# Weight split in 256-column pieces, sign folded into a selecting block, fewer input transfers, mean scaled on ScalarE, later value blocks first

## What is computed

```python
# stick-breaking: weights of a block of queries times the values
a = jnp.where(causal, jnp.exp(jax.nn.log_sigmoid(z) + rest), 0.0)
o = jnp.einsum('bhqk,bhkd->bhqd', a, v)
...
# matrix memory, gates: running sum b, and the running maximum of ig - b
b = jnp.cumsum(lfc, axis=-1)
log_d = b[..., :, None] - b[..., None, :] + igc[..., None, :]
m_t = jnp.maximum(jnp.max(log_d, axis=-1), log_inter)
d = jnp.exp(log_d - m_t[..., None])
...
def layer_norm(x, g, b):
    mu = jnp.mean(xf, axis=-1, keepdims=True)
    var = jnp.mean(jnp.square(xf - mu), axis=-1, keepdims=True)
    return (xf - mu) * lax.rsqrt(var + LN_EPS) * g + b
...
for i in range(2):
    x = layer_norm(ALPHA * x + mix, ...)
    x = layer_norm(ALPHA * x + jnp.square(jax.nn.relu(x @ w_up)) @ w_down, ...)
    x = x + jax.nn.sigmoid(x @ ple_w_gate + ple_b_gate) * (p @ ple_w_proj)
```

## Time and profile before

| | |
|---|---|
| median of 3 runs | 1488.28 us (1486.82 to 1488.86) |
| profiled execution | 1491.34 us, its span 1489.2 us |
| TensorE (PE) busy | 1475.4 us, 99% |
| VectorE (DVE) | 707.4 us, 48% |
| ScalarE (ACT) | 434.9 us, 29% |
| GpSimd (POOL) | 901.6 us, 61% |
| mean granted clock of TensorE | 0.999 |

### The profile page before, as it was taken

The page is one execution under the profiler, slowest core; times in us unless marked ns, Lnnn a source line. Parts: engine busy times, 40 slices in busy tenths (PEclk is TensorE's granted clock), DMA queues, the critical chain, the costliest instruction groups (busy, mean ns, idle before and its releaser), DMA issues.

```text
span 1489.2 us, 19731 instructions
## 1 busy us (share of the span) xinstructions
PE 1475.4 (99%) x7141; PEld 1198.9 (81%) x7150; DVE 707.4 (48%) x868; ACT 434.9 (29%) x880; POOL 901.6 (61%) x719
## 2 busy tenths in 40 slices
PE   9999999999999999999999999999999999999999
PEld 6888677878878888888888888877888888888887
DVE  6674658260036676103541183677777300552253
ACT  3242665141123422001210053766152100221032
POOL 7766035486633597667776656810659666777653
PEclk9999999999999999999999999999999999999999
DMA  6323011232221333333233322310323333333322
GB/s 207 113 86 107 16 43 62 80 113 84 89 69 43 99 99 110 93 94 98 99 99 99 95 65 96 123 35 15 99 68 116 99 99 94 93 97 99 99 85 85
DMA packets 37891, 132.72 MB, mean 89 GB/s; under 512 B 4368, under 2 KB 4800, under 8 KB 37824
## 3 DMA queue, kind: packets, MB, share of 16 engines
q1 hardware_dynamic: 37296, 130.39, 27.6%
q10 hardware_dynamic: 528, 1.36, 0.3%
HBM read 129.59 MB, written 2.10 MB: 88 GB/s over the span
## 4 chain that ended last, share of the span: by engine, by line
PE 94%; DVE 2%; ACT 2%; DMA 1%; POOL 0%; issue 0%; DVEq 0%; SPq 0%; ACTq 0%; POOLq 0%
PE PS L644 22%; PE PS L645 22%; PE PS L646 22%; PE PS L595 3%; PE PS L596 3%; PE PS L577 3%; PE PS L822 2%; PE PS L669 1%; PE PS L670 1%; PE PS L671 1%; PE PS L1099 1%; PE PS L914 1%; PE PS L929 1%; DMA W_raw<-in_weights 1%; PE PS L784 1%; PE PS L786 1%
## 5 line engine op out<-in xcount | busy, mean ns | idle before, releaser
L536 POOL TENSOR_TENSOR W_lo<-W_raw,W_hi 128x1024 fp32r<-128x1024 f32 x238 | 601.0, 2525 | 19.9
L533 POOL TENSOR_TENSOR HOLD<-HOLD 1x1 f32<-1x1 f32 x238 | 61.9, 260 | 550.9 <-PE PS L646 307.2
L644 PE MATMUL PS<-A_hi,W_hi 128*128 128x512 f32 x904 | 352.6, 390 | 0.0
L645 PE MATMUL PS<-A_hi,W_lo 128*128 128x512 f32 x904 | 351.9, 389 | 0.0
L646 PE MATMUL PS<-A_lo,W_hi 128*128 128x512 f32 x904 | 351.9, 389 | 0.0
L534 POOL TENSOR_SCALAR W_hi<-W_raw 128x1024 fp32r<-128x1024 f32 x238 | 247.3, 1039 | 0.0
L644 PE MATMUL PS<-H_hi,W_hi 128*128 128x512 f32 x512 | 199.2, 389 | 0.0
L645 PE MATMUL PS<-H_hi,W_lo 128*128 128x512 f32 x512 | 199.2, 389 | 0.0
L646 PE MATMUL PS<-H_lo,W_hi 128*128 128x512 f32 x512 | 199.2, 389 | 0.0
L644 PEld LDWEIGHTS PS<-A_hi,W_hi 128*128 128x128 f32 x904 | 170.0, 188 | 35.8 <-DVE A_lo L1733 0.5
L646 PEld LDWEIGHTS PS<-A_lo,W_hi 128*128 128x128 f32 x904 | 169.8, 188 | 35.4
(11 more groups left out here) (347 smaller groups left out, 2037.2 us busy)
## 6 DMA issues: line engine op xcount, KB each, us to landing
W_raw<-in_weights SPq DMA_DIRECT2D x238, 512.0 KB, 3.5
X<-in_x SPq DMA_DIRECT2D x8, 256.0 KB, 5.9
out<-X SPq DMA_DIRECT2D x7, 256.0 KB, 4.1
RELU<-in_ple_in ACTq DMA_DIRECT2D x2, 512.0 KB, 3.7
CONST<-in_constants SPq DMA_DIRECT2D x1, 849.5 KB, 8.8
PARAM<-in_params SPq DMA_DIRECT2D x1, 320.5 KB, 7.3
SIN<-in_positions ACTq DMA_DIRECT2D x1, 256.0 KB, 4.0
out<-X SPq DMA_DIRECT2D x2, 128.0 KB, 1.7
```

The lines of the kernel that those rows point to most:

```text
L533: pool.tensor_tensor(HOLD[:, 1 + s:2 + s], HOLD[:, 0:1], HOLD[:, 0:1], ALU.add)
L536: pool.tensor_tensor(W_lo[:, s, :], W_raw[:, r, :], W_hi[:, s, :].bitcast(F32), ALU.subtract).then_inc(w_lo, 1)
L644: pe.matmul(PS[:, bank, :], W_hi[:, slot, w], hi[:, kk, :], start=first, stop=False)
L645: pe.matmul(PS[:, bank, :], W_lo[:, slot, w], hi[:, kk, :], start=False, stop=False)
```

## The change

- `split`: the copy to `W_hi` and the subtraction to `W_lo` are each issued as four instructions of 256 columns (`W_PIECES`); the semaphores are set by the last piece.
- `X_PARTS` is 4 instead of 8: `X` comes in four transfers of two tiles each.
- Stick-breaking: a new semaphore `sb_att_later` is set after the exponential of blocks 1 to 3. TensorE waits for it first, multiplies blocks 1, 2, 3, then waits for `sb_att` and multiplies block 0.
- Layer norm: VectorE leaves the sum over features unscaled in `SMALL[:, 44:48]` and signals `tokens_summed`, for which it waits itself too; ScalarE scales it to the mean between `projected(0)` and `projected(1)` and signals `mean_held`; L2148 is gone. TensorE spreads the mean before `project(l, half, 2, 1)` instead of after it.
- Gates: `SELECT_B` is the block times -1, and `ROWS[:, 2, :]` is not negated any more.

```diff
--- before.py
+++ after.py
@@ -45,7 +45,8 @@
 QK_SCALE = HD ** -0.5
 NEG = -1e30
 RAW_SLOTS, W_SLOTS = 2, 4
-X_PARTS = 8
+W_PIECES = [slice(c * D // 4, (c + 1) * D // 4) for c in range(4)]
+X_PARTS = 4
 WOVEN = 3
 ACC = 4
 
@@ -305,7 +306,7 @@
         stats_done, mean_ready = sem("stats_done"), sem("mean_ready")
         var_ready, sd_ready = sem("var_ready"), sem("sd_ready")
         rstd_cols, rstd_ready = sem("rstd_cols"), sem("rstd_ready")
-        mean_cols, mean_held = sem("mean_cols"), sem("mean_held")
+        mean_cols, mean_held, tokens_summed = sem("mean_cols"), sem("mean_held"), sem("tokens_summed")
 
         centred, normed, x_ready, x_home = sem("centred"), sem("normed"), sem("x_ready"), sem("x_home")
         act_own, dve_own = sem("act_own"), sem("dve_own")
@@ -325,6 +326,7 @@
         angle_ready, angle_done = sem("angle_ready"), sem("angle_done")
 
         qk_sq, qk_lo, qk_ms, qk_sd, qk_normed = (sem("qk_" + n) for n in ("sq", "lo", "ms", "sd", "normed"))
+        sb_att_later = sem("sb_att_later")
         head_mean_in, minus_in = sem("head_mean_in"), sem("minus_in")
 
         fox_soft, fox_rows, fox_gates_in = sem("fox_soft"), sem("fox_rows"), sem("fox_gates_in")
@@ -531,10 +533,13 @@
                     pool.wait_ge(block_done, n - W_SLOTS + 1)
 
                 pool.tensor_tensor(HOLD[:, 1 + s:2 + s], HOLD[:, 0:1], HOLD[:, 0:1], ALU.add)
-                pool.tensor_scalar(W_hi[:, s, :], W_raw[:, r, :], 1.0, 1.0, ALU.mult, ALU.mult).then_inc(w_hi, 1)
+                for c in W_PIECES:
+                    done = pool.tensor_scalar(W_hi[:, s, c], W_raw[:, r, c], 1.0, 1.0, ALU.mult, ALU.mult)
+                done.then_inc(w_hi, 1)
                 pool.wait_ge(w_hi, n + 1)
-                pool.tensor_tensor(W_lo[:, s, :], W_raw[:, r, :], W_hi[:, s, :].bitcast(F32),
-                                   ALU.subtract).then_inc(w_lo, 1)
+                for c in W_PIECES:
+                    done = pool.tensor_tensor(W_lo[:, s, c], W_raw[:, r, c], W_hi[:, s, c].bitcast(F32), ALU.subtract)
+                done.then_inc(w_lo, 1)
 
             pool.memset(HOLD[:], 0.0).then_inc(hold_set, 1)
             pool.wait_ge(hold_set, 1)
@@ -1019,12 +1024,14 @@
                     add(SP_lo, 0).then_inc(sb_summed, 1)
 
                 def weigh(c):
-                    pe.wait_ge(sb_att, 2 * c + 2)
-                    for j in range(NT):
+                    pe.wait_ge(sb_att_later, 2 * c + 2)
+                    for j in (1, 2, 3, 0):
+                        if j == 0:
+                            pe.wait_ge(sb_att, 2 * c + 2)
                         for h in (2 * c, 2 * c + 1):
                             half = slice(h % 2 * HD, h % 2 * HD + HD)
                             mm = pe.matmul(PS[half, 6 + c, j * P:T], V1[:, j, 4 + c, half], packed(ATT, h % 2, j),
-                                           start=j == 0, stop=j == NT - 1, skip_group_check=True)
+                                           start=j == 1, stop=j == 0, skip_group_check=True)
                     mm.then_inc(sb_weighed, 1)
 
                 late = PLAN["late1"].before
@@ -1136,9 +1143,9 @@
                 turn_sums(SQSUM, 5).then_inc(stats_done, 1)
                 project(l, half, 1, 1)
                 project(l, half, 2, 0)
-                project(l, half, 2, 1)
                 pe.wait_ge(mean_held, n + 1)
                 spread_columns(MEAN_AT, 4).then_inc(mean_ready, 1)
+                project(l, half, 2, 1)
                 spread_rstd(n + 1)
                 project(l, half, 3, 0)
                 project(l, half, 3, 1)
@@ -1432,7 +1439,7 @@
                 def weights(h):
                     later = slice(PACKED_AT[1], PACKED)
                     act.wait_ge(sb_summed, 2 * h + 1)
-                    act.activation(ATT[:, h % 2, later], packed_scores(h)[:, later], ACT.Exp)
+                    act.activation(ATT[:, h % 2, later], packed_scores(h)[:, later], ACT.Exp).then_inc(sb_att_later, 1)
                     act.wait_ge(sb_summed, 2 * h + 2)
                     act.activation(packed(ATT, h % 2, 0), packed_scores(h, 0), ACT.Exp).then_inc(sb_att, 1)
 
@@ -1582,6 +1589,8 @@
                     act.activation(projection(4 * (n % 2) + i), PS[:, PROJECTION_BANKS[i], :], ACT.Copy).then_inc(by_act, 1)
 
                 projected(0)
+                act.wait_ge(tokens_summed, n + 1)
+                act.activation(SMALL[:, MEAN_AT:MEAN_AT + NT], SMALL[:, 44:48], ACT.Copy, scale=1.0 / D).then_inc(mean_held, 1)
                 projected(1)
                 act.wait_ge(var_ready, n + 1)
                 act.activation(SMALL[:, RSTD_AT:RSTD_AT + NT], SMALL[:, 56:60], ACT.Sqrt, bias=EPS_COL[:, 1:2]).then_inc(sd_ready, 1)
@@ -2126,7 +2135,7 @@
                     add_square_to(KD - 1)
 
             def layer_norm(n, stage_at):
-                mean, square, var = SMALL[:, MEAN_AT:MEAN_AT + NT], SMALL[:, 52:56], SMALL[:, 56:60]
+                total, square, var = SMALL[:, 44:48], SMALL[:, 52:56], SMALL[:, 56:60]
 
                 def scaled_low(k):
                     dve.wait_ge(x_ready, KD * n + k + 1)
@@ -2136,16 +2145,18 @@
                     dve.tensor_tensor(X[:, k, :], X[:, k, :], PS[:, 4, :], ALU.subtract).then_inc(centred, 1)
 
                 dve.wait_ge(mean_cols, n + 1)
-                own(dve.tensor_reduce(mean, PS[:, 7, :].rearrange("p (t c) -> p t c", t=NT), mybir.AxisListType.X, ALU.add))
+                dve.tensor_reduce(total, PS[:, 7, :].rearrange("p (t c) -> p t c", t=NT), mybir.AxisListType.X,
+                                  ALU.add).then_inc(tokens_summed, 1)
+                dve.wait_ge(tokens_summed, n + 1)
                 dve.wait_ge(stats_done, n + 2)
                 own(dve.tensor_reduce(var, PS[:, 5, :].rearrange("p (t c) -> p t c", t=NT), mybir.AxisListType.X, ALU.add))
                 own.wait()
-                own(dve.scalar_tensor_tensor(out=square, in0=mean, scalar=1.0 / (D * D), in1=mean, op0=ALU.mult, op1=ALU.mult))
+                own(dve.scalar_tensor_tensor(out=square, in0=total, scalar=1.0 / (D * D), in1=total, op0=ALU.mult,
+                                             op1=ALU.mult))
                 own.wait()
                 own(dve.scalar_tensor_tensor(out=var, in0=var, scalar=1.0 / D, in1=square, op0=ALU.mult, op1=ALU.subtract))
                 own.wait()
                 dve.tensor_scalar(var, var, 0.0, None, ALU.max).then_inc(var_ready, 1)
-                dve.tensor_scalar(mean, mean, 1.0 / D, None, ALU.mult).then_inc(mean_held, 1)
                 reciprocal_columns(n + 1)
                 dve.wait_ge(mean_ready, n + 1)
                 centre(0)
@@ -2206,7 +2217,7 @@
             def memory_gates():
                 fg = slice(32, 32 + M_HEADS)
                 own(dve.memset(PARTS_B[:], 0.0))
-                own(dve.tensor_copy(SELECT_B[:], const("select", row=slice(0, 68))))
+                own(dve.tensor_scalar(SELECT_B[:], const("select", row=slice(0, 68)), -1.0, None, ALU.mult))
                 dve.wait_ge(m_tanh, 1)
                 dve.tensor_scalar(MG[:, 2, :], MG[:, 1, :], CAP, None, ALU.mult).then_inc(m_capped, 1)
                 dve.wait_ge(m_soft, 1)
@@ -2220,9 +2231,6 @@
                 own(dve.tensor_tensor_scan(ROWS[:, 2, :], ROWS[:, 0, :], ROWS[:, 0, :], 0.0, ALU.max, ALU.max))
                 own.wait()
                 dve.tensor_tensor(ROWS[:, 3, :], ROWS[:, 1, :], ROWS[:, 2, :], ALU.add).then_inc(m_rows, 1)
-                dve.wait_ge(m_rows, 1)
-                own(dve.tensor_scalar(ROWS[:, 2, :], ROWS[:, 2, :], -1.0, None, ALU.mult))
-                own.wait()
                 own(dve.tensor_copy(PARTS_B[0:M_HEADS, :], ROWS[:, 2, :]))
                 own.wait()
                 own(dve.tensor_tensor(REST[fg, :], ROWS[:, 2, :], PARTS_B[0:M_HEADS, :], ALU.subtract))
```

## The result

The changed kernel takes 1502.93 us (median of 4 runs, 1502.68 to 1503.03) against 1488.57 (1486.82 to 1489.03) for the kernel before: ratio 1.0091, 95% interval 1.0078 to 1.0105. It is 14 us slower, where 5 us faster was forecast. The profiled execution has a span of 1501.2 us, 12.0 more than before.

A forecast was written before the change was run, and what follows sets the result against it. TensorE, busy 99% of the span, was taken as the bound, so only its standstills count: -4.1 - 1.1 - 0.4 + 0 + 0.3 = -5.3 us, giving 1483.0 us, range 1481.0 to 1487.3.

The forecast's parts named there:

- The split in pieces of 256 columns: GpSimd's weight split: six more instructions add 0.9 us a block, about 4.55 against TensorE's 5.44, hidden behind the matmuls.
- first MLP halves: Where VectorE and GpSimd exclude each other: a block takes 5.3 to 5.4 of 5.44 us, just covered, costed at nothing.
- rival A: First MLP halves: GpSimd becomes the bound at 0.26 us a piece, 15 us lost over 24 blocks, 1493 us; chance 9%.
- Gate stage: TensorE's wait for PARTS_B and the half clock behind it go once the negation is out: -4.1 us, bounds 1.2 to 4.1.
- Rival D: Gate stage: the stall stays, the chain only waits for the same POOL instructions; 1.2 instead of 4.1, 1485.9 us; chance 6%.
- +0.3 for the third weight block: Gate stage, woven start of qk2: the third block, needed three tiles later, costs 0.3 us, bounds 0 and 1.8.
- rival B: Gate stage: the stall moves to a weight block, 1.8 us instead of 0.3, 1484.5 us, 1486.2 if the clock falls; 16%.
- Norms: Four normalisations: spreading the mean one product earlier saves 0.27 us each, 1.1 us in all, bounds nothing to 1.6.
- Stick-breaking: TensorE's wait for the weights ATT: multiplying the later blocks first saves 0.4 us once, bounds 0.2 and 0.9.
- Start: Input in four transfers instead of eight: zero, bounds -0.5 and +0.8; W_raw(2) taken up before 17 us as sign.
- Sum: All terms together: -5.3 us, from 1491.34 us profiled to 1486.0, then 3.06 us off for the median: 1483.0.

The follow-up runs named there:

- experiment 1: The changed kernel with all its other edits, but the split in one piece of 1,024 columns again: 1485.22 us, ratio 0.9977 to the kernel before.
- experiment 8: The kernel before with only the sign moved into SELECT_B and the negation of the row removed: 1486.79 us, ratio 0.9980.

## Why the prediction was wrong

- **The failed step** is in "The split in pieces of 256 columns": "a block of about 4.55 us against TensorE's 5.44, hidden behind the matmuls". The 4.55 is right. These are GpSimd's rows after, in the stretch of the earlier trace rows where nothing disturbs it: a block takes 612.80 to 617.32, 4.52 us.

```profile
612.80 0.18 POOL L535 TENSOR_TENSOR HOLD<-HOLD 1x1 f32<-1x1 f32 x1
612.95 1.50 POOL L537 TENSOR_SCALAR W_hi<-W_raw 128x256 fp32r<-128x256 f32 x4
614.53 2.82 POOL L541 TENSOR_TENSOR W_lo<-W_raw,W_hi 128x256 fp32r<-128x256 f32 x4
617.32 0.18 POOL L535 TENSOR_TENSOR HOLD<-HOLD 1x1 f32<-1x1 f32 x1
```

  The other side, 5.44, is the wrong measure. It is TensorE's pace from tile to tile, and a woven start takes three blocks at once. The prediction worked that out for one such start (16.3 us for three tiles of `qk2`), but never for a start with another one five tiles ahead, where 4.0 us a block are to be had. Cost: 9.4 us of the 18.0 us between the kernel after and experiment 1. That the margin was nil stood in the trace before.
- **A mis-sized term**: in the first MLP halves the block was put at 5.3 to 5.4 us. The first three blocks behind the woven start took 5.8 to 6.2; GpSimd in `up0a`, after:

```profile
527.96 0.64 POOL L535 TENSOR_TENSOR HOLD<-HOLD 1x1 f32<-1x1 f32 x1
528.57 1.50 POOL L537 TENSOR_SCALAR W_hi<-W_raw 128x256 fp32r<-128x256 f32 x4
530.15 4.03 POOL L541 TENSOR_TENSOR W_lo<-W_raw,W_hi 128x256 fp32r<-128x256 f32 x4
534.15 0.18 POOL L535 TENSOR_TENSOR HOLD<-HOLD 1x1 f32<-1x1 f32 x1
```

  Four subtractions that take 2.82 us alone take 4.03, since VectorE takes a turn more than once within one block; "at most 0.1" for this was too little by 0.4 to 0.8 us, in these three blocks. From the fourth on a block took 5.3 to 5.4 us (545.39 to 550.69, for example), as predicted, and was not waited for. Two pieces of `W_lo` start 0.69 to 0.70 us apart where VectorE is idle, as forecast, and up to 1.15 in `up0a`, where over 0.75 was the sign of rival A. Rival A's place was right and its reason was not: the fixed part is 0.15 us, not 0.26. Its 15 us for 24 blocks were 3.2, since only three blocks in each half came late. Its time was also wrongly added: 1488.3 - 5.3 + 15 is 1498, not 1493. And the estimate of 5.5 us a block left out the 0.1 us that stands beside it; with it, it is 5.6.
- **Gate stage**: -4.1 predicted; -4.0 by the sign alone. Rival D fell; no stretch of half clock is left near 330. That the whole came was close: with whole blocks the chain from the first scan to its last step takes 17.3 us (308.27 to 325.60) instead of 19.8 (308.74 to 328.56), 2.5 less, where 2.36 were needed. The +0.3 for the third weight block was 0.7, rival B in small. Not seen: either edit alone removes the stall.
- **Norms**: -0.27 each predicted, -0.35 measured with whole blocks, and by the reason given. With pieces the waits moved to the reciprocal (L735 waits 1.3 us in all), and all four norms gave the gain back (0.1 to 0.5 us slower than before). TensorE and VectorE at the first, after:

```profile
502.71 0.65 PE L735 MATMUL PS<-CONST,SMALL 128*128 128x128 f32 x4 [0.62 <-DVE SMALL L1798]
```

```profile
500.83 0.58 DVE L2157 SCALAR_TENSOR_TENSOR SMALL<-SMALL 128x4 f32<-128x4 f32 x1
501.44 0.67 DVE L2159 TENSOR_SCALAR SMALL<-SMALL 128x4 f32<-128x4 f32 x1
```

  The prediction reckoned the variance chain as if GpSimd were idle, as it was before from 502.67 on, and did not look at where a slower GpSimd would stand.
- **Stick-breaking**: -0.4 predicted, -0.3 measured.
- **Start**: 0 predicted, and four transfers are worth nothing. `W_raw(2)` was not taken up before 17 us even with whole blocks (17.24, behind a wait for the data). With pieces the start is +1.1: the block was taken up at 17.84, not for lack of data, and its own split took 0.9 us longer. GpSimd came late by itself, because block 1's low part shared its time with VectorE's `R_lo`:

```profile
12.33 0.39 POOL L535 TENSOR_TENSOR HOLD<-HOLD 1x1 f32<-1x1 f32 x1 [2.19 <-DMA W_raw<-in_weights]
...
14.28 3.61 POOL L541 TENSOR_TENSOR W_lo<-W_raw,W_hi 128x256 fp32r<-128x256 f32 x4
17.84 0.18 POOL L535 TENSOR_TENSOR HOLD<-HOLD 1x1 f32<-1x1 f32 x1
```

- **Sum**: without the pieces' 0.3 the prediction has -5.6; measured in experiment 1 -6.0. The pieces were put at +0.3 and cost 18.0 us of span. A smaller error stands in the last step, which takes another 3.06 us off because the median of before is that far below its profiled execution. That execution is of the kind with the lower clock (experiment 8), and the gate term had already taken the clock's part off. 1491.34 - 5.6 is 1485.7, near the 1485.22 of experiment 1; with the 3.06 it would be 1482.7.

## What to carry to other kernels

An engine that feeds another is covered only if it meets the tightest demand, not the mean one. For each place where the consumer takes several blocks at once, count the blocks to be made since the last time that the slots were full, and the time until the last is needed; an engine at 61% busy had no margin at one such place. A cost added to the feeder is hidden where a block is ready well before it is taken, and lost one for one where it is taken as soon as it is ready. The old trace shows which: compare the two times.

Shorter instructions on an engine that shares access with another help the other one and slow their own; try them only where the other one is late.

## What was not expected of the hardware

- Six one-element additions on GpSimd cost a block 0.87 us where VectorE is idle (1.05 us for seven against 0.18 for one), and 1.50 us for seven at `rope3`: also an instruction on one element waits for VectorE's turn.
- Behind a single standstill of 2.10 us (two pieces, `rope3`) the granted clock stayed at 1.00; behind the 2.20 us of the earlier trace rows it had fallen to 0.50. The windows of the kernel with two pieces:

```profile
905.00:907.00 2.00, 0.24 (x2) 0.00 (x0) 1.39 (x2) 0.51 (x2) 2.00 (x2) 1.00 0.39 158
907.00:909.00 2.00, 1.66 (x7) 1.42 (x8) 1.81 (x4) 0.15 (x1) 1.94 (x4) 1.00 0.31 45
```

  What tells the two apart stays open. It is not the length of the standstill alone: ten executions of the kernel with two pieces have mean granted clocks from 0.997 (1491.20 us) to 1.000 (1488.16 us), so one and the same kernel seems to go both ways, as the kernel before does in experiment 8.
